# A chunked scan on TensorE: outputs of two chunks at a time, behind every second half tile, with a second weight buffer

## The chip, the cores and the metric

One core of a Trainium2 chip runs the whole kernel. The metric is the device time of one execution in microseconds (us), median of several runs. Lower is better.

## What is computed

The reference is two networks in a row, each of two layers. The change lies in the first layer of the second one, a Mamba-like mixer over T = 768 tokens (256 of a context and 512 of the input), cut into six chunks of 128, for 8 groups of 4 heads of 64. It is run forwards and backwards; per chunk, with `la_cum` the running sum of log decays:

```python
states = jnp.einsum('bcsgn,bcsgr,bcsgrp->bcgrpn', bc, to_end, xc)
...
decay = jnp.exp(jnp.where(causal, seg, -jnp.inf))
cb = jnp.einsum('bclgn,bcsgn->bclsg', cc, bc)
w = cb[..., None] * decay * dtc[:, :, None]
y_diag = jnp.einsum('bclsgr,bcsgrp->bclgrp', w, xc)
y_off = jnp.einsum('bclgn,bcgrpn,bclgr->bclgrp', cc, prev, jnp.exp(la_cum))
return (y_diag + y_off).reshape(xs.shape), final
```

The sum of both directions, plus a skip term, is multiplied by `silu(z)`, normed and multiplied by `out_w`.

## The kernel before

The kernel is written as one hand-ordered program for each engine; semaphores are the only links between them. TensorE (PE), VectorE (DVE), ScalarE (ACT) and GpSimd (POOL) each walk their own list, and an instruction that waits holds up all that is behind it on its engine.

The weights come in tiles of 1 MB. SyncE loads a tile into `wraw`, POOL splits it into a rounded part `whi` (L413) and a rest `wlo` (L417), and PE multiplies with whi-hi, wlo-hi and whi-lo (three matmuls for one product). POOL starts on a buffer when PE reports its old tile as done.

The mixer runs over the groups g: seven in a loop (`pe.Fori(0, GROUPS - 1)`, L1015, and its like on the other engines) and the eighth, `last`, written out. The scan of a group needs few PE instructions between long waits for DVE and ACT, so in the seven looped groups PE puts half tiles of the next group's projections between them. A half tile is 24 matmuls of 384 columns, half of the 768 tokens (`dense`, L825): x0, x1 (two feature blocks of x), b and c, each in two parts. The slots of L974 are, in order, x0 part 1, x1 part 0, x1 part 1, b part 0, b part 1, c part 0, and behind slot c PE does:

- `log_decay(c + 1)` (L939): sums of log decays into banks 4 and 5, once ACT has read those of chunk c;
- `off_part(c + 1)` (L950): the state's contribution into bank 6, once DVE has read that of chunk c (semaphore `offs_r`);
- `y_part(c)` (L954): two turned sums (L960), that is `offs` transposed into bank 7, then eight instructions for the four weighted products (L967), `xcb` against `wdec`, which write 64 partitions each and so have the form 128x64 where all others are 128x128. Bank 7 is used in halves by even and odd chunks.

ACT makes the exponentials of a chunk (`decays`, L1731, eight instructions into `ebuf`), copies finished projections out of PSUM (`copy_in`, L1644 to L1646), takes the tanh of the convolutions (L1650, L1651) and rounds the first and second half of the gated result (`u_hi`, L1739, which waits for the gates of three chunks). Its order is: decays(1), (2), (3), copy_in(1), tanh(0), decays(4), u_hi(0), decays(5), copy_in(2), u_hi(1), and so on.

DVE does per chunk c: `skip(c)` (L2519); `offsets(c)` (L2540 to L2544), which reads bank 6 and ends with the addition that lets PE go on with the off sums of the next chunk and the turned sums of this one; `gate_y(c)` (L2550), which multiplies the finished chunk in bank 7 by z; and `weights(c)` (L2525 the sum of both directions' decays, L2528 times C.B) into the one buffer `wdec`, which must wait for `y_part(c - 1)`. Between these it convolves the next group's projections: `conv_start`, four `conv_tap`s (L2388) and a `silu` (L2402) for each of four blocks b. Then come `u_lo` (L2559) and, in the output stage, `out_add` (L2621) into `oacc`.

Of the kernel before, what the change touches and what calls it, by code (L numbers as in the profile page):

```python
# [20 lines left out]
ALU = mybir.AluOpType  # L21
# [3 lines left out]
P = 128  # L25
# [74 lines left out]
def build(nc, io):  # L100
# [93 lines left out]
    btok = at("btok", 178.375, [P, NC, NS])  # L194
    xte = at("xte", 147.375, [P, NC, 2, HPG, HD])
    wdec = at("wdec", 184.375, [P, HPG, P])
    offs = at("offs", 186.375, [P, 3, HPG, HD])
    stmp = at("stmp", 199.875, [P, HPG, HD])
    acc = at("acc", 189.375, [P, T])
# [292 lines left out]
    def _(pe):  # L492
# [377 lines left out]
        def group(g, last):  # L870
# [83 lines left out]
            def y_part(c):  # L954
# [13 lines left out]
                                       start=False, stop=True, skip_group_check=(b == 1))  # L968
                mm.then_inc(y_ps, 1)

            log_decay(0)
            dense(T_G0 % 2, lambda i: i * TM + P, P, IN, EIGHT, True, 2, None)
            off_part(0)
            for c, (name, part) in enumerate((("x0", 1), ("x1", 0), ("x1", 1), ("b", 0), ("b", 1), ("c", 0))):  # L974
                next_half(name, part)
                if c + 1 < NC:
                    log_decay(c + 1)
                    off_part(c + 1)
                y_part(c)
            next_half("c", 1)  # L980

            k = 1 if last else 3
# [968 lines left out]
    def _(dve):  # L1951
# [516 lines left out]
        def group(g, last):  # L2468
# [46 lines left out]
            def skip(c):  # L2515
                if c:
                    dve.wait_ge(offs_r, g * 6 + c)
                dr = drow[:, bass.ds(g * HPG, HPG)].unsqueeze(2).broadcast_to([P, HPG, HD])
                k(V.tensor_tensor(stmp[:, :, :], x4(c), dr, ALU.mult))  # L2519

            def weights(c):
                dve.wait_ge(ex_r, g * 6 + (c + 1))
                if c:
                    dve.wait_ge(y_ps, g * 6 + c)
                V.tensor_tensor(wdec[:, :, :], ebuf[:, 0, :, :], ebuf[:, 1, :, :], ALU.add).then_inc(W_r, 1)  # L2525
                dve.wait_ge(W_r, g * 12 + 2 * c + 1)
                cb = xcb[:, c, 256:384].unsqueeze(1).broadcast_to([P, HPG, P])
                V.tensor_tensor(wdec[:, :, :], wdec[:, :, :], cb, ALU.mult).then_inc(W_r, 1)  # L2528

            def offsets(c):  # L2530
                dve.wait_ge(off_ps, g * 6 + (c + 1))
# [14 lines left out]
            def gate_y(c):  # L2546
# [4 lines left out]
                                       .rearrange("p (b n) -> p b n", b=2), scalar=0.5, in1=z,  # L2551
                                       op0=ALU.mult, op1=ALU.mult).then_inc(y_rd, 1)

            def u_lo(half):

                dve.wait_ge(uh_r, g * 2 + (half + 1))
# [4 lines left out]
                ins.then_inc(u_r, 1)  # L2561

            s1 = g + 1
            skip(0)
            weights(0)
            z_gate(1)
            dve.wait_ge(z_rd, g * 2 + 2)
            offsets(0)
            skip(1)
            offsets(1)  # L2570
            gate_y(0)
            if not last:
                load_params(s1, k)
            weights(1)
            if not last:
                conv_start(s1, 0, k)
                conv_tap(0, 1, k)
                conv_tap(0, 2, k)
            skip(2)
            offsets(2)  # L2580
            gate_y(1)
            weights(2)
            if not last:
                conv_tap(0, 3, k)
                conv_tap(0, 4, k)
            skip(3)
            offsets(3)
            gate_y(2)
            weights(3)
            if not last:  # L2590
                conv_start(s1, 1, k)
                conv_tap(1, 1, k)
            skip(4)
            offsets(4)
            gate_y(3)
            weights(4)
            if not last:
                silu(s1, 0)
                conv_tap(1, 2, k)
            skip(5)  # L2600
            offsets(5)
            gate_y(4)
            weights(5)
            u_lo(0)
            if not last:
                conv_tap(1, 3, k)
                conv_tap(1, 4, k)
            gate_y(5)
            u_lo(1)
            if not last:  # L2610
                silu(s1, 1)
            blk = g * 10 + (4 if last else 6)

# [471 lines left out]
```

## Time and profile before

| | |
|---|---|
| median of 3 runs | 2378.02 us (2377.7 to 2378.32) |
| the profiled execution | 2376.67 us |
| its span, first to last instruction | 2374.5 us |
| mean granted TensorE clock | 0.995 |
| PE busy | 2300.4 us (97%) |
| DVE busy | 1485.9 us (63%) |
| ACT busy | 757.8 us (32%) |
| POOL busy | 1437.1 us (61%) |
| the chain that ended last | PE 76%, DVE 16% |

A busy PE is one with a matmul under way. In a timeline, a row with a count stands for that many instructions in a row, from the start of the first to the end of the last, and neighbouring matmuls overlap; so the distance of two starts tells what one costs. "[0.28 <-DVE wdec L2528]" is idle time before the instruction and what ended it. The seven looped groups of the mixer take about 90 us each, from 1316 us on; their rows repeat to within some hundredths of a microsecond.

### The profile page before, as it was taken

What the parts mean: (1) busy time and instruction counts of PE and PEld (TensorE: products, weight loads), DVE (VectorE), ACT (ScalarE), POOL (GpSimd) and SP (SyncE); (2) the same over time, 40 slices, a digit from 0 to 9 for tenths busy, and PEclk for the clock granted to TensorE, in tenths of its full rate; (3) what the DMA queues carried; (4) which work ended last, traced back from release to release, by engine and by line L of the source; (5) the groups of instructions that cost most, each with busy time, mean ns of one, the idle gap of its engine ahead of it and who ended that gap; (6) DMA issues with size and microseconds to landing.
All of it is one profiled execution on the core that took longest, in us unless ns stands there. A gap on an engine that the chain in (4) does not pass through costs nothing.

```text
span 2374.5 us, 32220 instructions
## 1 busy us (share of the span) xinstructions
PE 2300.4 (97%) x11638; PEld 1901.1 (80%) x11638; DVE 1485.9 (63%) x1851; ACT 757.8 (32%) x1582; POOL 1437.1 (61%) x1259
## 2 busy tenths in 40 slices
PE   8999999999999999999999999999999998999998
PEld 6768888888777788888878899999999986776447
DVE  7965343444774543343468889789789788536653
ACT  3453210112333420110246333333333333532551
POOL 8737776778776477776876434344344341365885
PEclk9999999999999999999999999999999998999999
DMA  4321434433224033443332111110111112122212
GB/s 167 107 81 71 149 135 147 149 132 123 89 76 129 36 131 135 160 142 132 117 115 107 37 53 35 53 53 35 53 53 35 53 53 83 34 74 76 54 27 71
DMA packets 41596, 211.31 MB, mean 89 GB/s; under 512 B 5408, under 2 KB 9504, under 8 KB 21536
## 3 DMA queue, kind: packets, MB, share of 16 engines
q1 hardware_dynamic: 27456, 164.84, 19.7%
q10 hardware_dynamic: 14048, 45.17, 5.8%
q8 instruction: 67, 1.10, 0.2%
q14 instruction: 25, 0.20, 0.0%
HBM read 197.67 MB, written 7.34 MB: 86 GB/s over the span
## 4 chain that ended last, share of the span: by engine, by line
PE 76%; DVE 16%; issue 3%; ACT 2%; DMA 1%; POOL 1%; ACTq 0%; DVEq 0%; SPq 0%; POOLq 0%
PE ps L528 40%; PE ps L825 14%; PE ps L1077 5%; DVE convd L2388 3%; PE ps L1188 2%; PE ps L1170 1%; PE ps L927 1%; PE ps L1175 1%; DVE wdec L2525 1%; PE ps L622 1%; PE ps L950 1%; DVE convd L2402 1%; PE ps L1133 1%; DVE convd L2384 1%; DVE offs L2542 1%
## 5 line engine op out<-in xcount | busy, mean ns | idle before, releaser
L413 POOL TENSOR_SCALAR whi<-wraw 128x512 fp32r<-128x512 f32 x564 | 386.6, 714 | 869.0 <-PE ps L825 374.3
L417 POOL TENSOR_TENSOR wlo<-wraw,whi 128x512 fp32r<-128x512 f32 x568 | 859.4, 1543 | 0.8 <-ACT whi L1428 0.8
L528 PE MATMUL ps<-uhi,whi 128*128 128x512 f32 x896 | 353.6, 395 | 16.1 <-POOL wlo L390 11.6
L528 PE MATMUL ps<-uhi,wlo 128*128 128x512 f32 x896 | 349.9, 390 | 0.0
L528 PE MATMUL ps<-ulo,whi 128*128 128x512 f32 x896 | 349.8, 390 | 0.0
L825 PE MATMUL ps<-inhi,whi 128*128 128x384 f32 (+1 forms) x784 | 242.8, 344 | 4.3 <-DVE inlo L2343 3.2
L825 PE MATMUL ps<-inlo,whi 128*128 128x384 f32 (+1 forms) x784 | 235.8, 335 | 0.0
L825 PE MATMUL ps<-inhi,wlo 128*128 128x384 f32 (+1 forms) x784 | 235.5, 335 | 0.0
L528 PEld LDWEIGHTS ps<-uhi,whi 128*128 128x128 f32 x896 | 168.8, 188 | 54.8 <-POOL wlo L390 11.6
L528 PE MATMUL ps<-hidhi,whi 128*128 128x512 f32 x512 | 199.4, 390 | 0.0
L528 PE MATMUL ps<-hidlo,whi 128*128 128x512 f32 x512 | 199.4, 390 | 0.0
L528 PE MATMUL ps<-hidhi,wlo 128*128 128x512 f32 x512 | 199.4, 389 | 0.0
L2224 DVE TENSOR_TENSOR h<-h,ps 128x1024 f32<-128x1024 f32 x40 | 48.9, 1221 | 239.3 <-PE ps L528 239.3
L528 PEld LDWEIGHTS ps<-uhi,wlo 128*128 128x128 f32 x896 | 168.8, 188 | 36.0 <-issue 1.4
L528 PEld LDWEIGHTS ps<-ulo,whi 128*128 128x128 f32 x896 | 168.7, 188 | 35.2
L1524 ACT ACTIVATE hsq<-hm 128x1024 f32<-128x1024 f32 x32 | 34.1, 1065 | 488.2 <-DVE hm L2255 488.2
L825 PEld LDWEIGHTS ps<-inhi,whi 128*128 128x128 f32 (+1 forms) x784 | 143.6, 187 | 15.6 <-issue 8.6
L2388 DVE SCALAR_TENSOR_TENSOR convd<-raw,cpg,convd 128x770 f32<-128x770 f32 x128 | 149.7, 1169 | 3.4 <-ACT convd L1631 0.9
L2255 DVE SCALAR_TENSOR_TENSOR hm<-ps,rstd 128x1024 f32<-128x1024 f32 x32 | 39.2, 1225 | 173.3 <-PE ps L528 173.2
L825 PEld LDWEIGHTS ps<-inhi,wlo 128*128 128x128 f32 (+1 forms) x784 | 144.2, 187 | 0.8
L825 PEld LDWEIGHTS ps<-inlo,whi 128*128 128x128 f32 (+1 forms) x784 | 144.1, 187 | 0.6
L1731 ACT ACTIVATE ebuf<-ps,tabg 128x128 f32<-128x128 f32 x384 | 104.4, 387 | 116.8 <-PE ps L939 83.8
(448 smaller groups left out, 4623.0 us busy)
## 6 DMA issues: line engine op xcount, KB each, us to landing
wraw<-in_wstream SPq DMA_DIRECT2D x150, 1024.0 KB, 4.8
modraw<-in_modw ACTq DMA_DIRECT2D x48, 512.0 KB, 3.3
hspill<-hres ACTq DMA_DIRECT2D x1, 3072.0 KB, 9.7
hback<-hspill ACTq DMA_DIRECT2D x1, 3072.0 KB, 10.1
Q<-qrow SPq DMA_DIRECT2D x24, 128.0 KB, 2.3
h<-in_x ACTq DMA_DIRECT2D x2, 1024.0 KB, 5.3
crow<-in_crow ACTq DMA_DIRECT2D x2, 1024.0 KB, 4.9
QL<-qrest SPq DMA_DIRECT2D x14, 128.0 KB, 2.3
```

Of the source, the lines that this page charges most:

```text
L413: pool.tensor_scalar(whi[:, s, c], wraw[:, s, c], 1.0, 0.0, ALU.mult, ALU.add).then_inc(wraw_read, 1)
L417: ins = pool.tensor_tensor(wlo[:, s, c], wraw[:, s, c], whi[:, s, c].bitcast(F32), ALU.subtract)
L528: mm = pe.matmul(ps[:, 2 * bank + m, :], a[:, w, c:c + P], b[:, kb, :], start=(n == 0 and i == 0), stop=(n == KB - 1 and i == 2))
L622: pe.matmul(ps[:, SCORE_BANKS(n)[c], 0:w], q, proj[64 * c:64 * c + 64, K0 + hd, 0:w], start=True, stop=False)
L825: mm = pe.matmul(ps[0:width, q + half, 0:HALF], a[:, s, c:c + width], b[:, kb, half * HALF:(half + 1) * HALF], start=(n == 0), stop=(n == ...
L1077: mm = pe.matmul(ps[:, q + m, :], a[:, k % 2, c:c + P], b[:, kb, t0:t0 + S], start=(kb == 0 and i == 0), stop=(kb == KB - 1 and i == 2))
L1188: mm = pe.matmul(ps[64 * e:64 * e + 64, 2, :], vtok2[:, kb, HD * j:HD * j + HD], pT2[(NC * b + kb) % RING][:, e, :], start=(kb == 0), stop ...
L1524: A(hsq[n % 2][:, :, :], hm[n % 2][:, :, :], ACT.Square).then_inc(L["sqh_r"], 1)
L1731: ins = A(ebuf[:, d, r, :], ps[:, 4 + d, r * P:(r + 1) * P], ACT.Exp, bias=tabg[:, K_NB + 2 * c + d, r:r + 1])
L2224: V.tensor_tensor(h[:, 2 * j:2 * j + 2, :], h[:, 2 * j:2 * j + 2, :], TWO(bank), ALU.add).then_inc(L["h_r"], 1)
L2255: V.scalar_tensor_tensor(out=hm[n % 2][:, :, :], in0=TWO(n % 2), scalar=0.0, in1=rstd2, op0=ALU.max, op1=ALU.mult).then_inc(L["m_r"], 1)
L2388: ins = V.scalar_tensor_tensor(out=o, in0=r[:, n:n + CW], scalar=cpg[:, 6 * b + n:6 * b + n + 1], in1=o, op0=ALU.mult, op1=ALU.add)
```

## The change

In the looped groups PE no longer computes outputs behind every half tile. Behind the slots of the odd chunks (1, 3, 5) it does both chunks of a pair: the four turned sums first (`y_turn`), then the sixteen instructions of weighted products (`y_dec`). A pair fills bank 7, so it waits until the gate of the pair before has been read. The odd chunk's weights have a buffer of their own, `wdec1`, in space that `ul` uses later, so `weights(c)` waits only for the pair before its own. One `gate_pair` of 512 elements per partition takes the place of two `gate_y` of 256. DVE's list gets a new order: `load_params` stands where `gate_y(0)` was; `gate_pair(0)`, `(2)` and `(4)` stand behind `offsets(2)`, behind `offsets(4)` and behind `u_lo(0)`; `silu(s1, 0)` and `conv_tap(1, 2)` move from behind `weights(4)` to ahead of `skip(4)`; `conv_tap(1, 3)` and `(1, 4)` move from behind `u_lo(0)` to ahead of `skip(5)`. ACT's and POOL's lists stay. The last group keeps the old code. The diff, cut by the branch that repeats the old DVE order for the last group:

```diff
     btok = at("btok", 178.375, [P, NC, NS])
     xte = at("xte", 147.375, [P, NC, 2, HPG, HD])
     wdec = at("wdec", 184.375, [P, HPG, P])
+    wdec1 = at("wdec1", 154.875, [P, 2, T])[:, :, 0:2 * P].rearrange("p a (r n) -> p a r n", r=2)
     offs = at("offs", 186.375, [P, 3, HPG, HD])
     stmp = at("stmp", 199.875, [P, HPG, HD])
     acc = at("acc", 189.375, [P, T])
@@ -968,6 +969,34 @@
                                        start=False, stop=True, skip_group_check=(b == 1))
                 mm.then_inc(y_ps, 1)
 
+            def y_turn(c):
+
+                pe.wait_ge(offs_r, g * 6 + (c + 1))
+                for b in range(2):
+                    q = b * 256 + c % 2 * P
+                    pe.matmul(ps[:, 7, q:q + P], offs[:, 2 * (c % 2), 2 * b:2 * b + 2, :].rearrange("p r n -> p (r n)"), ident[:, :],
+                              start=(q == 0), stop=False, skip_group_check=(q > 0), is_transpose=True)
+
+            def y_dec(c):
+
+                pe.wait_ge(W_r, g * 12 + 2 * c + 2)
+                for b in range(2):
+                    q = b * 256 + c % 2 * P
+                    for r in range(2):
+                        x0 = (2 * b + r) * HD
+                        w = wdec1[:, b, r, :] if c % 2 else wdec[:, 2 * b + r, :]
+                        mm = pe.matmul(ps[64 * r:64 * r + 64, 7, q:q + P], xcb[:, c, x0:x0 + HD], w,
+                                       start=False, stop=True, skip_group_check=(q > 0))
+                mm.then_inc(y_ps, 1)
+
+            def y_pair(c):
+
+                pe.wait_ge(y_rd, g * 6 + (6 + c))
+                y_turn(c)
+                y_turn(c + 1)
+                y_dec(c)
+                y_dec(c + 1)
+
             log_decay(0)
             dense(T_G0 % 2, lambda i: i * TM + P, P, IN, EIGHT, True, 2, None)
             off_part(0)
@@ -976,7 +1005,10 @@
                 if c + 1 < NC:
                     log_decay(c + 1)
                     off_part(c + 1)
-                y_part(c)
+                if last:
+                    y_part(c)
+                elif c % 2:
+                    y_pair(c - 1)
             next_half("c", 1)
 
             k = 1 if last else 3
@@ -2520,12 +2552,17 @@
 
             def weights(c):
                 dve.wait_ge(ex_r, g * 6 + (c + 1))
-                if c:
+                if last and c:
                     dve.wait_ge(y_ps, g * 6 + c)
-                V.tensor_tensor(wdec[:, :, :], ebuf[:, 0, :, :], ebuf[:, 1, :, :], ALU.add).then_inc(W_r, 1)
+                elif c > 1:
+                    dve.wait_ge(y_ps, g * 6 + c - 1)
+                own = c % 2 == 0 or last
+                w = wdec[:, :, :].rearrange("p (a r) n -> p a r n", a=2) if own else wdec1
+                e = lambda d: ebuf[:, d, :, :].rearrange("p (a r) n -> p a r n", a=2)
+                V.tensor_tensor(w, e(0), e(1), ALU.add).then_inc(W_r, 1)
                 dve.wait_ge(W_r, g * 12 + 2 * c + 1)
-                cb = xcb[:, c, 256:384].unsqueeze(1).broadcast_to([P, HPG, P])
-                V.tensor_tensor(wdec[:, :, :], wdec[:, :, :], cb, ALU.mult).then_inc(W_r, 1)
+                cb = xcb[:, c, 256:384].unsqueeze(1).unsqueeze(1).broadcast_to([P, 2, 2, P])
+                V.tensor_tensor(w, w, cb, ALU.mult).then_inc(W_r, 1)
 
             def offsets(c):
                 dve.wait_ge(off_ps, g * 6 + (c + 1))
@@ -2551,6 +2588,13 @@
                                        .rearrange("p (b n) -> p b n", b=2), scalar=0.5, in1=z,
                                        op0=ALU.mult, op1=ALU.mult).then_inc(y_rd, 1)
 
+            def gate_pair(c):
+
+                dve.wait_ge(y_ps, g * 6 + (c + 2))
+                z = zs[:, :, c * P:(c + 2) * P]
+                V.scalar_tensor_tensor(out=z, in0=ps[:, 7, :].rearrange("p (b n) -> p b n", b=2), scalar=0.5, in1=z,
+                                       op0=ALU.mult, op1=ALU.mult).then_inc(y_rd, 2)
+
             def u_lo(half):
 
                 dve.wait_ge(uh_r, g * 2 + (half + 1))
@@ -2561,53 +2605,73 @@
                 ins.then_inc(u_r, 1)
 
             s1 = g + 1
...
+            else:
+                skip(0)
+                weights(0)
+                z_gate(1)
+                dve.wait_ge(z_rd, g * 2 + 2)
+                offsets(0)
+                skip(1)
+                offsets(1)
                 load_params(s1, k)
-            weights(1)
-            if not last:
+                weights(1)
                 conv_start(s1, 0, k)
                 conv_tap(0, 1, k)
                 conv_tap(0, 2, k)
-            skip(2)
-            offsets(2)
-            gate_y(1)
-            weights(2)
-            if not last:
+                skip(2)
+                offsets(2)
+                gate_pair(0)
+                weights(2)
                 conv_tap(0, 3, k)
                 conv_tap(0, 4, k)
-            skip(3)
-            offsets(3)
-            gate_y(2)
-            weights(3)
-            if not last:
+                skip(3)
+                offsets(3)
+                weights(3)
                 conv_start(s1, 1, k)
                 conv_tap(1, 1, k)
-            skip(4)
-            offsets(4)
-            gate_y(3)
-            weights(4)
-            if not last:
                 silu(s1, 0)
                 conv_tap(1, 2, k)
-            skip(5)
-            offsets(5)
-            gate_y(4)
-            weights(5)
-            u_lo(0)
-            if not last:
+                skip(4)
+                offsets(4)
+                gate_pair(2)
+                weights(4)
                 conv_tap(1, 3, k)
                 conv_tap(1, 4, k)
-            gate_y(5)
-            u_lo(1)
-            if not last:
+                skip(5)
+                offsets(5)
+                weights(5)
+                u_lo(0)
+                gate_pair(4)
+                u_lo(1)
                 silu(s1, 1)
             blk = g * 10 + (4 if last else 6)
 
```

## Rows read from the trace of the kernel before

**Rows 1.** Waits of PE, 1345 to 1435 us; line <- who was waited for: us, times, longest.

```profile
PE ps L967 <- DVE wdec L2528: 0.3, 1, 0.3
PE ps L825 <- DVE oacc L2621: 0.2, 1, 0.2
```

**Rows 2.** Timeline of PE, second group: start us, us, instruction, count [idle before].

```profile
1435.34 0.38 PE L960 MATMUL ps<-ident,offs 128*128 128x128 f32 x2
...
1436.52 0.34 PE L825 MATMUL ps<-inhi,wlo 128*128 128x384 f32 x1
...
1440.51 0.63 PE L939 MATMUL ps<-lablk,lapick 128*128 128x512 f32 x2
1440.98 1.02 PE L950 MATMUL ps<-ast,ck 128*128 128x256 f32 x4
1441.84 0.38 PE L960 MATMUL ps<-ident,offs 128*128 128x128 f32 x2
1442.15 0.66 PE L967 MATMUL ps<-wdec,xcb 128*64 128x128 f32 x8
1442.74 0.44 PE L825 MATMUL ps<-inhi,whi 128*128 128x384 f32 x1
1443.02 0.34 PE L825 MATMUL ps<-inhi,wlo 128*128 128x384 f32 x1
```

**Rows 3.** Instructions of line L967: count, duration in ns min/median/max, start, forms.

```profile
L967 PE MATMUL ps<-wdec,xcb x384: 272/273/476, 1345.5 to 1994.5; 128*64 128x128 f32 x192
```

**Rows 4.** Timeline of PE, the last weighted products of the second group.

```profile
1466.52 0.38 PE L960 MATMUL ps<-ident,offs 128*128 128x128 f32 x2
1467.18 0.66 PE L967 MATMUL ps<-wdec,xcb 128*64 128x128 f32 x8 [0.28 <-DVE wdec L2528]
```

**Rows 5.** Busy time of each engine in a stretch: us, PE, PEld, DVE, ACT, POOL, clock, DMA.

```profile
1436.88:1467.50 30.62, 30.34 (x190) 27.74 (x191) 29.76 (x43) 12.93 (x45) 10.82 (x9) 1.00 0.20 68
```

**Rows 6.** Timeline of DVE, second group.

```profile
1450.80 0.41 DVE L2550 SCALAR_TENSOR_TENSOR zs<-ps,zs 128x256 f32<-128x256 f32 x1
1451.13 1.45 DVE L2525 TENSOR_TENSOR wdec<-ebuf 128x512 f32<-128x512 f32 x1
1452.62 1.66 DVE L2528 TENSOR_TENSOR wdec<-wdec,xcb 128x512 f32<-128x512 f32 x1
...
1459.48 0.42 DVE L2544 TENSOR_TENSOR offs<-offs,stmp 128x256 f32<-128x256 f32 x1
...
1461.48 0.95 DVE L2402 SCALAR_TENSOR_TENSOR convd<-raw,convd 128x770 f32<-128x770 f32 x1
...
1463.40 0.42 DVE L2519 TENSOR_TENSOR stmp<-xcb,drow 128x256 f32<-128x256 f32 x1
...
1466.43 0.69 DVE L2528 TENSOR_TENSOR wdec<-wdec,xcb 128x512 f32<-128x512 f32 x1
...
1468.10 2.07 DVE L2388 SCALAR_TENSOR_TENSOR convd<-raw,cpg,convd 128x770 f32<-128x770 f32 x2
1470.09 0.42 DVE L2550 SCALAR_TENSOR_TENSOR zs<-ps,zs 128x256 f32<-128x256 f32 x1
```

**Rows 7.** Groups of DVE instructions: count | busy us, mean ns | idle before, releaser.

```profile
L2474 DVE SCALAR_TENSOR_TENSOR zs<-zs,ps 128x768 f32<-128x768 f32 x16 | 15.3, 954 | 30.2 <-ACT zs L1699 30.2
...
L2550 DVE SCALAR_TENSOR_TENSOR zs<-ps,zs 128x256 f32<-128x256 f32 x48 | 19.9, 415 | 0.0
```

**Rows 8.** Timeline of ACT, second group.

```profile
1435.08 0.50 ACT L1646 ACTIVATE raw<-ps 128x384 f32<-128x384 f32 x1
...
1441.26 2.17 ACT L1731 ACTIVATE ebuf<-ps,tabg 128x128 f32<-128x128 f32 x8 [3.62 <-PE ps L939]
...
1456.27 1.17 ACT L1739 ACTIVATE uh<-zs,mng 128x384 fp32r<-128x384 f32 x2
```

**Rows 9.** Timeline of PE in the last group (g = 7).

```profile
1973.23 0.67 PE L950 MATMUL ps<-ast,ck 128*128 128x256 f32 x2 [2.09 <-DVE offs L2544]
```

**Rows 10.** Busy time of each engine in a stretch of the last group.

```profile
1974.80:1978.00 3.20, 3.00 (x7) 1.85 (x8) 3.13 (x5) 0.32 (x2) 3.20 (x3) 0.50 1.00 430
```

More of the change, by code:

```diff
@@ L2563, in group @@
             s1 = g + 1
[L2564 to L2571, printed above, removed]
-            if not last:
+            if last:
+                skip(0)
[5 more added lines that the diff above has]
+                offsets(1)
+                gate_y(0)
+                weights(1)
+                skip(2)
+                offsets(2)
+                gate_y(1)
+                weights(2)
+                skip(3)
+                offsets(3)
+                gate_y(2)
+                weights(3)
+                skip(4)
+                offsets(4)
+                gate_y(3)
+                weights(4)
+                skip(5)
+                offsets(5)
+                gate_y(4)
+                weights(5)
+                u_lo(0)
+                gate_y(5)
+                u_lo(1)
+            else:
+                skip(0)
+                weights(0)
+                z_gate(1)
+                dve.wait_ge(z_rd, g * 2 + 2)
+                offsets(0)
+                skip(1)
+                offsets(1)
                 load_params(s1, k)
-            weights(1)
-            if not last:
+                weights(1)
                 conv_start(s1, 0, k)
@@ L2578, in group @@
                 conv_tap(0, 2, k)
-            skip(2)
-            offsets(2)
-            gate_y(1)
-            weights(2)
-            if not last:
+                skip(2)
+                offsets(2)
+                gate_pair(0)
+                weights(2)
                 conv_tap(0, 3, k)
                 conv_tap(0, 4, k)
-            skip(3)
-            offsets(3)
-            gate_y(2)
-            weights(3)
-            if not last:
+                skip(3)
+                offsets(3)
+                weights(3)
                 conv_start(s1, 1, k)
                 conv_tap(1, 1, k)
-            skip(4)
-            offsets(4)
-            gate_y(3)
-            weights(4)
-            if not last:
                 silu(s1, 0)
                 conv_tap(1, 2, k)
-            skip(5)
-            offsets(5)
-            gate_y(4)
-            weights(5)
-            u_lo(0)
-            if not last:
+                skip(4)
+                offsets(4)
+                gate_pair(2)
+                weights(4)
                 conv_tap(1, 3, k)
                 conv_tap(1, 4, k)
-            gate_y(5)
-            u_lo(1)
-            if not last:
+                skip(5)
+                offsets(5)
+                weights(5)
+                u_lo(0)
+                gate_pair(4)
+                u_lo(1)
                 silu(s1, 1)
```

## The prediction

> **What bounds the kernel now.** The page comes first: TensorE (PE) is busy 97% of the span, so time can only come from work it stops doing, or go into idle time it is given. The waits of PE over one scan iteration are small; two matter here [rows 1]. One is 0.3 us on the second write of `wdec` (L2528): VectorE (DVE) hands over the last chunk's weights just after PE wants them. The timeline of PE gives the rhythm [rows 2]: a half tile of 24 matmuls runs at (1440.51 - 1436.52) / 23 = 0.173 us each, 4.16 us; the decay sums cost 0.47 (L939 to L950) and the two off sums 0.86 (L950 to L960). From 1436.88 to 1467.50 DVE is busy 29.76 of 30.62 us [rows 5]: from `gate_y(0)` to the end of `weights(5)` it does nothing but follow its own list. Two engines are thus both nearly full, and DVE's list ends last [rows 4]. A change that moves DVE work ahead of `weights(5)` is paid by PE.
>
> **PE's part.** No matmul is added or removed. What goes is the change of form between the 128x128 and the 128x64 matmuls. Of one `y_part` [rows 2]: one matmul of 128 columns lasts 0.273 [rows 3]; the two turned sums last 0.38 together, so they start 0.11 apart and need 0.22; the first weighted product starts 0.31 after the first turned sum, 0.09 lost. The eight product instructions last 0.66 together, so they start 0.055 apart, 0.44; the next L825 starts 0.59 after the first, 0.15 lost. The L825 after that comes 0.28 later and not 0.173, 0.11 lost. Lost in all: 0.35 us for each group of products. Three groups instead of six save 3 x 0.35 = 1.05 us per iteration, if PE is what counts. A pair costs 2 x 0.66 + 0.35 = 1.67 us.
>
> **DVE's part.** Compare the two lists up to the end of `weights(5)`.
> - Out: five `gate_y` (chunks 0 to 4). One holds its slot for 1451.13 - 1450.80 = 0.33 us [rows 6], five 1.67.
> - In: two `gate_pair`, 512 elements. The nearest rows are the same operation on 256 elements, 0.415, and one of the same kind on 768, 0.954 [rows 7]: 0.27 per further 256, so the slot is 0.33 + 0.27 = 0.60, two 1.20. Bounds: 0.33 (nothing for the length) and 0.69 with no overlap with the next instruction.
> - In: `conv_tap(1, 3)` and `conv_tap(1, 4)`, which stood behind `weights(5)` and now stand ahead of `skip(5)`: 1470.09 - 1468.10 = 1.99 us [rows 6].
> - `silu(s1, 0)` and `conv_tap(1, 2)` stay ahead of `weights(5)` but now stand ahead of `skip(4)`: nothing for this sum, 1463.40 - 1461.48 = 1.92 for `offsets(4)` [rows 6].
> - The weights go to `wdec` or `wdec1` with the same 512 elements: I take no cost. Bounds 0 and, for a poorer access pattern, 0.05 on each of six instructions (no row shows one; 0.05 is about half of the overlap that a gate has, 0.415 less 0.33).
> Sum: -1.67 + 1.20 + 1.99 = +1.52 us until `weights(5)` is ready. No wait ahead of it is later: the chain is free of PE between those points except where checked below.
>
> **The timeline this makes**, in the second group, that of the rows. After the off sum of chunk 1, PE would go straight on at 1435.34 (where L960 starts now), but x1 writes the bank that ScalarE (ACT) copies out until 1435.08 + 0.50 = 1435.58 [rows 8]: a new wait of 0.3, start 1435.65 with 0.1 for the start. Then half tile 4.16, 1.33 for decay and off sums, pair 1.67, half tile, 1.33, half tile, 1.33, pair, half tile: 1459.7. The pair (2, 3) finds its weights: `weights(3)` ended at 1452.62 + 1.66 = 1454.28 [rows 6], is now 0.4 earlier (three gates out, one pair in), and PE comes to it at about 1454.9.
> Then `off_part(5)`: after 0.47 of L939 PE is there at 1460.2 and waits for `offsets(4)`, which ended at 1459.48 + 0.42 = 1459.90 [rows 6] and now ends at 1459.90 + 1.92 - 3 x 0.33 + 0.60 = 1461.4. **New stall, 1.2 to 1.3 us**, L950 on L2544; queued behind it are `off_part(5)`, the half tile c and everything after. PE leaves at 1461.5, off sums 0.86, c 4.16: 1466.5. That is where it was before (L960 at 1466.52 [rows 4]): the 1.2 us it had gained is gone.
> The pair (4, 5) now waits for `offsets(5)` and then for `weights(5)`: ready before at about 1467.12 (1466.43 + 0.69 [rows 6]), now at 1468.64. PE could take it at 1466.5 + 0.97 = 1467.5. It starts the products of chunk 5 at 1468.70 instead of 1467.18 [rows 4] and the next half tile 1.52 us later than before. ACT's last exponentials don't stand in for this: `u_hi(0)` now waits for `gate_pair(2)` (about 1462.1), its 1.17 and the 2.2 of eight exponentials [rows 8] end at 1465.4, before DVE comes to `weights(5)` at 1467.2.
>
> **Behind the scan.** PE waits 0.2 us for DVE's first sum into `oacc` [rows 1]. `u_lo(1)` and what follows on DVE start when they did before (the taps are done, `gate_pair(4)` starts at about 1469.7, where `gate_y(5)` was at 1470.09), while PE is 1.5 later: this wait goes, 0.18 back. POOL's split of the next tile starts later with PE; `wsplit` is not among PE's waits [rows 1]. The unrolled last group keeps its old order.
> Per iteration 1.52 - 0.18 = +1.34 us, seven iterations 9.4 us. The profiled execution took 2376.67 us (span 2374.5 and 2.2 around it), 1.35 under the median of the three runs: 2376.7 + 9.4 = 2386.1, and against the median **2387.4 us**.
>
> **Clock.** In the last group PE stood idle 2.09 us on this same pair of lines, and 1.6 us later its clock was granted at half, 1.2 GHz, from 1974.8 to 1978.0 [rows 9, 10]. The forecast adds one stall of 1.3 us and two of about 0.6 per iteration. No row of the loop shows so much, so I take no drop. The Trainium skill says (TensorE: Matmul & The Clock Gate, "A second HAM failure mode: psum-queue depth-cycling") that short idle times between groups of matmuls can make the clock swing; the last group agrees with it, and by that rule the second rival below would be the result.
>
> **Rivals.**
> - *Faster: PE's saving counts.* If DVE had `weights(5)` ready by the time PE comes, PE would keep its 1.05 and lose the 0.3 wait of now, less 0.3 for ACT's bank: about 1.0 us per iteration, 2378 - 7 = 2371. It decides where DVE's list is over 1.1 us shorter than I make it and its `offsets(4)` too. For it: PE is 97% busy. Against: two taps of 1.0 each are plainly ahead of the weights. Chance 0.10.
> - *Slower still: the clock drops in the loop.* Some 3.2 us at half clock lose 1.6, of which the later waits may hide 1.1 if it falls early: 0.5 to 1.6 more per iteration, 2391 to 2399, I take 2396. Chance 0.08.
> - *No difference.* The stalls are eaten where PE has other waits, or the idle of PE lets DVE and POOL, which slow each other (L2528 1.66 us at 1452.62, 0.69 at 1466.43 [rows 6]), meet less: with half a microsecond to 1.3 per iteration given back, 2378 to 2382. Chance 0.12.
> - The forecast has 0.70; its own range is 2383 to 2392 (gates and access patterns move 1.34 by -0.5 to +0.7 per iteration).
> The range 2377 to 2396 leaves out the faster rival and the top of the slower one. About 0.2% (4.8 us) is what a measurement can tell from no change: faster 0.10, same 0.12, slower 0.78.
>
> **What would show it.** In the profile after: PE's waits get L950 on DVE L2544 with 1.2 to 1.5 us in each of seven iterations (nothing of the kind before outside the last group), the transposes and products of the last pair wait for `offs` and `wdec` by about 0.6 each, and one wait of 0.3 on the copy L1646 appears; the gaps between forms halve in number; the wait on `oacc` is gone in the loop; each of the seven iterations grows by 1.3 us; the clock stays at 1.00. It is wrong if DVE is idle ahead of `weights(5)`, if the stall before `off_part(5)` is missing, or if `gate_pair` takes much other than 0.68.

## The result, and the profile after

The changed kernel takes 2391.4 us (median of 4 runs, 2389.9 to 2393.5) against 2378.2 before: 1.0056 times as long (95% interval 1.0044 to 1.0068), 13.2 us more, where 9.4 were forecast. The profiled execution took 2390.2 us with a span of 2388.2, 13.7 over the span of before, at a mean granted clock of 0.993. Line numbers shift: L825, L937, L939 and L950 are now L826, L938, L940 and L951; the turned sums are L977, the weighted products L988; on DVE `weights` is L2562 and L2565, `offsets` L2577 to L2581, `gate_pair` L2595, taps L2420, `silu` L2434, `out_add` L2685.

PE's waits in the second group, 1437 to 1527 us (those of [rows 1] are of the first):

```profile
PE ps L951 <- DVE offs L2581: 1.9, 1, 1.9
PE ps L938 <- ACT ast L1754: 0.6, 1, 0.6
PE ps L988 <- DVE wdec L2565: 0.3, 1, 0.3
PE ps L977 <- DVE offs L2581: 0.3, 1, 0.3
```

The 0.6 on L938 was there before (L937). New are the stall before `off_part(5)` and 0.3 on the turned sums; the 0.3 on `wdec` stays; the wait on `oacc` is gone.

The timeline of PE in the first group (as [rows 2, 4]; a start 0.12 lower than before is the same moment, as L940 at 1344.21 and L939 at 1344.33 tell):

```profile
1344.68 0.59 PE L951 MATMUL ps<-ast,ck 128*128 128x256 f32 x2
1345.40 0.44 PE L826 MATMUL ps<-inhi,whi 128*128 128x384 f32 x1
...
1351.00 0.60 PE L977 MATMUL ps<-ident,offs 128*128 128x128 f32 x4
1351.53 1.09 PE L988 MATMUL ps<-wdec,xcb 128*64 128x128 f32 x16
1352.56 0.44 PE L826 MATMUL ps<-inhi,whi 128*128 128x384 f32 x1
...
1372.00 1.10 PE L951 MATMUL ps<-ast,ck 128*128 128x256 f32 x4 [1.90 <-DVE offs L2581]
...
1377.12 0.38 PE L977 MATMUL ps<-ident,offs 128*128 128x128 f32 x2
1377.80 0.44 PE L977 MATMUL ps<-ident,offs 128*128 128x128 f32 x2 [0.30 <-DVE offs L2581]
1378.17 0.66 PE L988 MATMUL ps<-wdec,xcb 128*64 128x128 f32 x8
1379.13 0.66 PE L988 MATMUL ps<-wdec,xcb 128*64 128x128 f32 x8 [0.30 <-DVE wdec L2565]
1379.72 0.44 PE L826 MATMUL ps<-inhi,whi 128*128 128x384 f32 x1
```

The pair starts at 1351.00 and the half tile behind it at 1352.56, 1.56, and its second matmul follows 0.11 late: 1.67. The half tile behind the last products starts at 1379.72. In the kernel before it was this one:

```profile
1377.66 0.44 PE L825 MATMUL ps<-inhi,whi 128*128 128x384 f32 x1
```

so PE is 1379.72 - 1377.66 + 0.12 = 2.18 us late there, not 1.52. The timeline of DVE after, same group (as [rows 6]):

```profile
1346.64 1.26 DVE L2406 COPY cpg<-p 128x24 f32 x1
...
1354.08 0.68 DVE L2595 SCALAR_TENSOR_TENSOR zs<-ps,zs 128x512 f32<-128x512 f32 x1
1354.68 0.68 DVE L2562 TENSOR_TENSOR wdec<-ebuf 128x512 f32<-128x512 f32 x1
...
1360.85 1.78 DVE L2562 TENSOR_TENSOR wdec<-ebuf 128x512 f32<-128x512 f32 x1
1362.66 1.64 DVE L2565 TENSOR_TENSOR wdec<-wdec,xcb 128x512 f32<-128x512 f32 x1
...
1367.86 0.96 DVE L2434 SCALAR_TENSOR_TENSOR convd<-raw,convd 128x770 f32<-128x770 f32 x1
1368.73 1.01 DVE L2420 SCALAR_TENSOR_TENSOR convd<-raw,cpg,convd 128x770 f32<-128x770 f32 x1
...
1378.38 0.69 DVE L2565 TENSOR_TENSOR wdec<-wdec,xcb 128x512 f32<-128x512 f32 x1
```

Beside it the same list of the kernel before, where two gates stand, of chunk 0 and of chunk 2:

```profile
1346.75 0.41 DVE L2550 SCALAR_TENSOR_TENSOR zs<-ps,zs 128x256 f32<-128x256 f32 x1
1347.08 0.94 DVE L2374 COPY cpg<-p 128x24 f32 x1
...
1360.69 0.41 DVE L2550 SCALAR_TENSOR_TENSOR zs<-ps,zs 128x256 f32<-128x256 f32 x1
1361.03 1.44 DVE L2525 TENSOR_TENSOR wdec<-ebuf 128x512 f32<-128x512 f32 x1
1362.50 1.66 DVE L2528 TENSOR_TENSOR wdec<-wdec,xcb 128x512 f32<-128x512 f32 x1
1364.09 1.63 DVE L2384 TENSOR_SCALAR convd<-raw,cpg 128x770 f32<-128x770 f32 x1
1365.75 1.93 DVE L2388 SCALAR_TENSOR_TENSOR convd<-raw,cpg,convd 128x770 f32<-128x770 f32 x1
...
1376.33 0.69 DVE L2528 TENSOR_TENSOR wdec<-wdec,xcb 128x512 f32<-128x512 f32 x1
```

and what POOL does at that time, before (L417) and after (L418):

```profile
1342.43 5.56 POOL L417 TENSOR_TENSOR wlo<-wraw,whi 128x512 fp32r<-128x512 f32 x4
...
1360.47 6.39 POOL L417 TENSOR_TENSOR wlo<-wraw,whi 128x512 fp32r<-128x512 f32 x4
```

```profile
1360.62 6.38 POOL L418 TENSOR_TENSOR wlo<-wraw,whi 128x512 fp32r<-128x512 f32 x4
```

Here is the missing 0.66 us. The `wlo` work of POOL runs in four instructions of 6.39 / 4 = 1.60 us, and meanwhile DVE gets one instruction done for each of them: L2525, L2528, L2384 and the first tap start 1.47, 1.59 and 1.66 apart, though with POOL idle they take 0.7 to 1.0.

The copy of `load_params` ends with POOL's last piece as well (1347.08 + 0.94 = 1348.02 against 1342.43 + 5.56 = 1347.99; after, 1346.64 + 1.26 = 1347.90 against 1347.86). With the gate in front of it taken away, the copy starts 0.32 earlier on the scale of before, lasts 0.32 longer (0.94 to 1.26) and ends where it did. `weights(1)` starts at 1347.94 + 0.12 = 1348.06 where it started at 1348.05.

For chunk 2 the list is already 0.27 late, because the first pair's gate takes 0.60 us in the place of 0.33. L2525 starts at 1360.85 + 0.12 = 1360.97, 0.06 earlier than before, but takes 1.78 instead of 1.44, and L2528 starts 1362.66 + 0.12 - 1362.50 = 0.28 late. So the missing gate of chunk 2 gave nothing back. POOL's pieces begin 1360.62 + 0.12 - 1360.47 = 0.27 later too: the two engines shift together. Of the five gates of 0.33 only three were worth anything.

The Trainium skill has a rule for such pairs (SBUF — State Buffer, "SBUF: two separate sides"): a VectorE operation with two SBUF inputs, while GpSimd reads SBUF, or one in a two-port mode, shares a port pair with GpSimd; whichever starts first holds it for its whole instruction, and the other waits. The rows agree in the pace of `weights` and the tap, one for each piece of 1.60 us. The copy and `conv_start` have one tensor input in SBUF and were held too; whether they ran in such a two-port mode no run here shows.

What the loop costs follows from the distance between the same instruction (L913 before, L914 after) in neighbouring groups: 90.11 us before; 91.84 in five of the seven groups after and 92.43 in two. 5 x 1.73 + 2 x 2.32 = 13.3 of the 13.7 us of span. The two slower groups hold a spell at the lower clock. Here is one of them (columns as in [rows 10]); the other shows 0.57 from 1832 to 1836, and the same place in the second group, 1463 to 1467, shows 1.00:

```profile
1647.00:1651.00 4.00, 3.41 (x10) 3.09 (x11) 3.92 (x6) 2.92 (x10) 0.00 (x0) 0.59 0.00 0
```

### The profile page after: what moved, and what is told of

It reads as the page before. It is cut to its first block, busy times and chain, and to the rows that moved or that the text cites. A ratio compares the mean times of both kernels' runs of the same rounds, so it can differ in the third digit from the quotient of the medians.

```text
span 2388.2 us, 32213 instructions
## 1 busy us (share of the span) xinstructions
PE 2300.0 (96%) x11638; PEld 1903.6 (80%) x11638; DVE 1499.2 (63%) x1830; ACT 758.3 (32%) x1582; POOL 1426.7 (60%) x1259
## 4 chain that ended last, share of the span: by engine, by line
PE 82%; DVE 10%; issue 3%; ACT 2%; POOL 1%; DMA 1%; ACTq 0%; DVEq 0%; SPq 0%; POOLq 0%
PE ps L529 41%; PE ps L826 18%; PE ps L1109 5%; DVE convd L2420 2%; PE ps L1220 2%; PE ps L1202 1%; PE ps L928 1%; PE ps L596 1%; POOL wlo L418 1%; DVE wdec L2562 1%; PE ps L1207 1%; PE ps L623 1%; PE ps L951 1%; PE ps L1165 1%; PE ps L1076 1%
## 5 line engine op out<-in xcount | busy, mean ns | idle before, releaser
L418 POOL TENSOR_TENSOR wlo<-wraw,whi 128x512 fp32r<-128x512 f32 x568 | 849.1, 1527 | 0.8 <-ACT whi L1460 0.8
L826 PE MATMUL ps<-inhi,whi 128*128 128x384 f32 (+1 forms) x784 | 245.0, 347 | 5.2 <-DVE inlo L2375 3.2
L826 PE MATMUL ps<-inhi,wlo 128*128 128x384 f32 (+1 forms) x784 | 236.1, 336 | 0.0
L826 PE MATMUL ps<-inlo,whi 128*128 128x384 f32 (+1 forms) x784 | 236.0, 335 | 0.0
L826 PEld LDWEIGHTS ps<-inhi,whi 128*128 128x128 f32 (+1 forms) x784 | 144.7, 188 | 16.4 <-DVE inlo L2375 5.8
L2420 DVE SCALAR_TENSOR_TENSOR convd<-raw,cpg,convd 128x770 f32<-128x770 f32 x128 | 155.4, 1214 | 3.4 <-ACT convd L1663 0.9
L826 PEld LDWEIGHTS ps<-inhi,wlo 128*128 128x128 f32 (+1 forms) x784 | 145.0, 188 | 1.3
L826 PEld LDWEIGHTS ps<-inlo,whi 128*128 128x128 f32 (+1 forms) x784 | 144.7, 187 | 0.6
```

The costliest lines, as they stand in the source:

```text
L418: ins = pool.tensor_tensor(wlo[:, s, c], wraw[:, s, c], whi[:, s, c].bitcast(F32), ALU.subtract)
L826: mm = pe.matmul(ps[0:width, q + half, 0:HALF], a[:, s, c:c + width], b[:, kb, half * HALF:(half + 1) * HALF], start=(n == 0), stop=(n == ...
L2420: ins = V.scalar_tensor_tensor(out=o, in0=r[:, n:n + CW], scalar=cpg[:, 6 * b + n:6 * b + n + 1], in1=o, op0=ALU.mult, op1=ALU.add)
```

## The experiments

Each ratio is against runs of the kernel before on the same chip, which took 2378.1 us beside all but the last three kernels and 2376.8 beside those. "Period" is the distance between neighbouring looped groups in the profiled execution.

**The moved convolution steps alone.** The kernel before, with its gates and single outputs, and only the four steps moved.

```diff
+                silu(s1, 0)
+                conv_tap(1, 2, k)
             skip(4)
             offsets(4)
             gate_y(3)
             weights(4)
             if not last:
-                silu(s1, 0)
-                conv_tap(1, 2, k)
+                conv_tap(1, 3, k)
+                conv_tap(1, 4, k)
             skip(5)
...
             u_lo(0)
-            if not last:
-                conv_tap(1, 3, k)
-                conv_tap(1, 4, k)
             gate_y(5)
```

> The kernel before with single outputs, but with the four conv steps moved as in the change: silu(s1, 0) and conv_tap(1, 2) ahead of skip(4), conv_tap(1, 3) and (1, 4) ahead of skip(5). Theory, VectorE's list ends last: weights(5) is 1.99 us later, PE gets back 0.47 behind the scan, so +1.5 us per looped group, about 2378 + 11 = 2389, perhaps 1 more where the clock falls. Rival, the pairing itself is what costs (its wait for a whole bank, its stalls): within 2 us of 2378.

Measured: 2388.5 us, ratio 1.0042 (1.0029 to 1.0056); period 91.65, +1.53. PE's waits in the second group:

```profile
PE ps L950 <- DVE offs L2544: 1.3, 1, 1.3
PE ps L967 <- DVE wdec L2528: 0.6, 2, 0.4
```

So 1.53 of the 1.73 us a group come without any pair, as expected. The two taps are the term, 1.99 less 0.46 given back behind the scan: 1.53. With these four steps moved, the pairs then add 91.84 - 91.65 = 0.19. A stall of 1.3 us came in each group and the clock did not fall in the loop.

**The pairs alone.** The change, with the four steps back where they stood.

```diff
-                silu(s1, 0)
-                conv_tap(1, 2, k)
                 skip(4)
                 offsets(4)
                 gate_pair(2)
                 weights(4)
-                conv_tap(1, 3, k)
-                conv_tap(1, 4, k)
+                silu(s1, 0)
+                conv_tap(1, 2, k)
                 skip(5)
                 offsets(5)
                 weights(5)
                 u_lo(0)
+                conv_tap(1, 3, k)
+                conv_tap(1, 4, k)
                 gate_pair(4)
```

> The changed kernel with pairs, second buffer and pair gates, but all four conv steps back at their old places. Theory: weights(5) only 0.2 us later than in the kernel before (three gates of 0.33 out, two pair gates of 0.60 in), PE bound to it as before: 2378 to 2380; the saving of PE between forms doesn't show. Rival 1, PE's saving counts: 2378 - 7 = 2371. Rival 2, the pairing costs: 2389 or more.

Measured: 2388.3 us, ratio 1.0046 (1.0032 to 1.0059); period 91.59. A miss by 8 us; the rival that the pairing costs (2389 or more) came nearer. `weights(5)` ends 0.16 late, close to the 0.2 of the sum, and the half tile behind it starts 0.16 late. The rest comes behind the scan, a wait on `oacc` seven times as long as before ([rows 1]):

```profile
PE ps L826 <- DVE oacc L2685: 1.5, 1, 1.5
```

The timeline of DVE there (starts 0.79 higher than before are the same moment), below it that of the kernel before, and last that of the change (0.12 lower):

```profile
1382.81 1.51 DVE L2603 SCALAR_TENSOR_TENSOR ul<-zs,mng,uh 128x384 fp32r<-128x384 f32 x2 [1.19 <-ACT uh L1771]
...
1386.53 3.21 DVE L2420 SCALAR_TENSOR_TENSOR convd<-raw,cpg,convd 128x770 f32<-128x770 f32 x2
1389.87 0.96 DVE L2685 TENSOR_TENSOR oacc<-oacc,ps 128x768 f32<-128x768 f32 x1
```

```profile
1381.59 1.15 DVE L2559 SCALAR_TENSOR_TENSOR ul<-zs,mng,uh 128x384 fp32r<-128x384 f32 x2 [1.19 <-ACT uh L1739]
...
1384.96 2.53 DVE L2388 SCALAR_TENSOR_TENSOR convd<-raw,cpg,convd 128x770 f32<-128x770 f32 x2
1387.63 0.95 DVE L2621 TENSOR_TENSOR oacc<-oacc,ps 128x768 f32<-128x768 f32 x1
```

```profile
1381.93 1.15 DVE L2603 SCALAR_TENSOR_TENSOR ul<-zs,mng,uh 128x384 fp32r<-128x384 f32 x2 [1.19 <-ACT uh L1771]
...
1384.58 2.54 DVE L2420 SCALAR_TENSOR_TENSOR convd<-raw,cpg,convd 128x770 f32<-128x770 f32 x2
1387.37 0.95 DVE L2685 TENSOR_TENSOR oacc<-oacc,ps 128x768 f32<-128x768 f32 x1 [0.26 <-PE ps L826]
```

The gate of the last pair is 0.27 longer and the scan 0.16 later, so `u_lo(1)` starts 1382.81 - 0.79 - 1381.59 = 0.43 late. It takes 1.51 instead of 1.15, and the two taps, which meet POOL's next `wlo` pieces (2.0 us each), last 3.21 instead of 2.53. The first sum starts 1389.87 - 0.79 - 1387.63 = 1.45 late. The pairs spare DVE nothing that counts there, and the list behind the scan had no slack: its wait of 0.2 said so.

In the change `u_lo(1)` is just as late, 1381.93 + 0.12 - 1381.59 = 0.46. But PE comes to its output stage 2.0 us later than here, and POOL, which starts its next split when PE reports, starts at 1384.49 on the scale of before where it started at 1382.45 here. `u_lo(1)`, `silu`, `conv_start` and the two taps then take 1.15, 0.95, 0.68 and 2.54 us, where here they take 1.51, 1.36, 0.97 and 3.21, and the first sum waits for PE. So it is PE's own lateness that took the wait on `oacc` away, and not an earlier list of DVE. The two halves don't add up (1.48 and 1.53 give 1.73 together), since PE pays for one late list at one place or the other.

**`silu` and one tap back, the last two taps left in front.**

```diff
-                silu(s1, 0)
-                conv_tap(1, 2, k)
                 skip(4)
                 offsets(4)
                 gate_pair(2)
                 weights(4)
+                silu(s1, 0)
+                conv_tap(1, 2, k)
                 conv_tap(1, 3, k)
```

> The changed kernel with only silu(s1, 0) and conv_tap(1, 2) back behind weights(4); conv_tap(1, 3) and (1, 4) stay ahead of skip(5). Theory: the 1.9 us stall of PE ahead of off_part(5) goes, but weights(5) comes at the same time, so PE waits there instead: 1.74 us per group as in the changed kernel, less the two clock drops of 0.58: 2390. Rival, the stall ahead of off_part(5) is the cost: 7 x 1.9 = 13 us less, 2378.

Measured: 2393.2 us, ratio 1.0066 (1.0052 to 1.008), 3 us over the forecast, which took no spells at half clock. The stall before `off_part(5)` is gone and stands whole before the turned sums of chunk 5:

```profile
PE ps L977 <- DVE offs L2581: 2.2, 1, 2.2
```

The period is 91.84 in four groups, the same as after the change to the hundredth, so the place of the stall doesn't matter: the end of `weights(5)` does. Three groups have a spell at half clock (the clock was 0.57 in 1379 to 1383) and take 92.8 to 92.9.

**Are the gates of chunks 0 and 2 free?** The kernel before, with the first put behind the held copy and the second behind both instructions of `weights(3)`. (In the last group both stay where they were; those lines of the edit are left out.)

```diff
-            gate_y(0)
             if not last:
                 load_params(s1, k)
+                gate_y(0)
...
-            gate_y(2)
             weights(3)
             if not last:
+                gate_y(2)
```

> The kernel before with two instructions of VectorE swapped in order, no work changed: gate_y(0) behind load_params in place of ahead of it, gate_y(2) behind weights(3) in place of ahead of it. Theory, the copy of load_params and the first sum of weights(3) are held until an instruction of POOL ends, so a gate ahead of them is free and one behind them costs 0.33: +0.66 us per looped group for weights(5), 7 x 0.66 = +4.6, about 2383. Rival, POOL only slows what runs beside it and order doesn't matter: 2378, within 1 us.

Measured: 2381.5 us, ratio 1.0016 (1.0007 to 1.0025); period 90.64, +0.53. The timeline of DVE:

```profile
1348.31 1.26 DVE L2374 COPY cpg<-p 128x24 f32 x1
1349.60 0.42 DVE L2550 SCALAR_TENSOR_TENSOR zs<-ps,zs 128x256 f32<-128x256 f32 x1
```

No work is added, the copy is 0.32 longer and everything behind the gate is 0.34 late: for chunk 0 the gate was free where it stood. For chunk 2 the test isn't clean: `y_part(3)` now waits 1.1 us for the late gate, and POOL's pieces fall on other instructions. L2525 went from 1.44 to 1.78 here too, but it starts 1.12 us later than before, so it is not the same meeting. `weights(5)` ends 0.50 late, between the 0.33 of one free gate and the 0.66 of two. For chunk 2 the rows of the change above are the better evidence.

**One sum earlier.** The pairs alone, with `out_add(0)` one tap earlier.

```diff
                 conv_tap(2, 1, k)
-                conv_tap(2, 2, k)
                 out_add(0)
+                conv_tap(2, 2, k)
                 conv_tap(2, 3, k)
```

> Pairs with the four conv steps at their old places, as in e2_pairs_conv_back (2388.3 us, 1.49 us idle per group before PE's fourth output block, waiting for VectorE's first sum into oacc), and now that first sum stands one conv tap earlier. Theory, only the lateness of that sum made the run before slow: the idle goes, 91.6 per group falls to 90.0 to 90.2, 2377 to 2379. Rival, the loss is somewhere else and only shows there: 2386 to 2388.

Measured: 2387.9 us, ratio 1.0042 (1.0027 to 1.0057); period 91.53. A miss: the wait of 1.4 us went to the next sum, which stands behind two taps of 2.98 us. A single place was not the cause; the list as a whole is late.

**The list behind the scan in another order, with pairs and without.** From `weights(5)` on, the taps 2 to 4 of block 1 go behind the last gate, the sums go one or two steps forward each, and the last three taps of block 3 behind the last sum. Once on the changed kernel, whose edit follows (cut behind the third sum), and once on the kernel before (with its `gate_y`s).

```diff
-                silu(s1, 0)
-                conv_tap(1, 2, k)
                 skip(4)
                 offsets(4)
                 gate_pair(2)
                 weights(4)
-                conv_tap(1, 3, k)
-                conv_tap(1, 4, k)
+                silu(s1, 0)
                 skip(5)
                 offsets(5)
                 weights(5)
                 u_lo(0)
                 gate_pair(4)
+                conv_tap(1, 2, k)
+                conv_tap(1, 3, k)
+                conv_tap(1, 4, k)
                 u_lo(1)
...
                 conv_start(s1, 2, k)
+                out_add(0)
                 conv_tap(2, 1, k)
+                out_add(1)
                 conv_tap(2, 2, k)
-                out_add(0)
+                out_add(2)
```

> Pairs with VectorE's list put in another order: conv_tap(1, 2), (1, 3) and (1, 4) between gate_pair(4) and u_lo(1), silu(s1, 0) behind weights(4), each sum into oacc one or two conv steps earlier. Theory: weights(5) is ready before PE comes, so PE keeps its 1.05 us between forms, less 0.3 for ACT's bank, and the wait for oacc of 0.47 goes: 88.8 to 89.2 per group, 2378 - 7 x 1.1 = 2370. Rival, VectorE's whole list is the bound and an order can't help: 2378 or more.

> The kernel before, single outputs, with the same new order of the conv steps and sums as e6_pairs_rebalanced. Theory: the waits for weights(5) (0.28) and for oacc (0.47) go, the form changes stay: 89.3 to 89.5 per group, 2378 - 7 x 0.7 = 2373; so e6 less e7 is what the pairing itself gives, 2 to 4 us. Rival, the pairing gives nothing: e6 and e7 within 1 us.

Measured: with pairs 2369.2 us, ratio 0.9962 (0.9948 to 0.9976), period 88.83; with single outputs 2370.4 us, ratio 0.9967 (0.9956 to 0.9978), period 89.27. In both, one wait of PE is left in a group, the 0.6 us for ACT that was there before.

So DVE's list bounds the kernel before and the changed one, and it is its order that decides. With one tap fewer ahead of `weights(5)` than even the kernel before, PE sets the pace almost alone, and the pairs are worth 0.44 a group. Almost: with pairs `off_part(5)` still starts 0.57 us behind its decay sums (1372.71 to 1373.28) where 0.47 is usual. Which of the two moves, the taps or the sums, brought how much was not tried. The whole times don't tell the two kernels apart, their intervals overlap: the first group of the profiled execution with pairs came 2.8 us later (L914 at 1328.41, L913 at 1325.59), by what happened ahead of the loop. The period does: it repeats to some hundredths from group to group in both.

**POOL's pieces halved.** The kernel before; in the scan's loop POOL writes `wlo` in eight instructions of 256 columns.

```diff
-                    ins = pool.tensor_tensor(wlo[:, s, c], wraw[:, s, c], whi[:, s, c].bitcast(F32), ALU.subtract)
+                    for m in range(parts):
+                        w = TILE // PIECES // parts
+                        c = slice((n * parts + m) * w, (n * parts + m + 1) * w)
+                        ins = pool.tensor_tensor(wlo[:, s, c], wraw[:, s, c], whi[:, s, c].bitcast(F32), ALU.subtract)
...
-            split_pair(i)
+            split_pair(i, parts=2)
```

> The kernel before with one change on POOL: in the scan's loop the rest of a tile (wlo) is made in eight instructions of 256 columns, not four of 512. Theory, an instruction of VectorE with two SBUF inputs is held until POOL's instruction beside it ends, one for each: four of them that take 1.45 to 1.93 us now take 0.8 to 1.2, weights(5) is ready some 2 us earlier, the two waits of 0.28 and 0.47 go: 2378 - 5 = 2373. Rival, they share a path in proportion and the size of a piece doesn't matter: 2378.

Measured: 2371.9 us, ratio 0.9972 (0.9962 to 0.9981), period 89.26. The timelines of DVE and POOL, second group (as [rows 6]):

```profile
1452.26 0.89 DVE L2528 TENSOR_TENSOR wdec<-ebuf 128x512 f32<-128x512 f32 x1
1453.18 1.11 DVE L2531 TENSOR_TENSOR wdec<-wdec,xcb 128x512 f32<-128x512 f32 x1
1454.22 1.10 DVE L2387 TENSOR_SCALAR convd<-raw,cpg 128x770 f32<-128x770 f32 x1
1455.35 1.37 DVE L2391 SCALAR_TENSOR_TENSOR convd<-raw,cpg,convd 128x770 f32<-128x770 f32 x1
```

```profile
1451.69 8.08 POOL L420 TENSOR_TENSOR wlo<-wraw,whi 128x256 fp32r<-128x256 f32 x8
```

The same four operations that took 1.45, 1.66, 1.63 and 1.93 take 0.89, 1.11, 1.10 and 1.37, in the rhythm of POOL's pieces of 8.08 / 8 = 1.01 us. POOL is slower in all (8.1 instead of 6.4 us), which nobody waits for. Because it works longer, three more operations of DVE meet it (`skip(4)` and two of `offsets(4)`, 0.83 to 0.84 us where they took 0.43), so `weights(5)` ends 0.88 us earlier and not the 2 us of the forecast. That was enough: both waits are gone. The length of POOL's instruction is what DVE pays.

**Halves with the change, and with both other orders.**

> The changed kernel as it is, with POOL's rest of a tile in eight instructions of 256 columns in the scan's loop. Theory: weights(5) comes about 1.0 us earlier, as it did in e8_pool_halves, of the 2.17 that it came later by the change: 91.84 per group falls to about 90.8, the stall ahead of off_part(5) from 1.9 to 0.9, no clock drops in the loop: 2383. Rival, the stalls and not VectorE's list set the time: 2390.

> Pairs in the new order of e6_pairs_rebalanced (88.83 per group, 2369.2) with POOL's halves on top. Theory: PE has no wait on VectorE left there, so a shorter list of VectorE brings nothing: 88.8 per group, 2369. Rival, both add up: 2363 to 2366.

> Singles in the new order of e7_singles_rebalanced (89.27 per group, 2370.4) with POOL's halves on top. Theory: 89.27 again, and 0.44 more per group than e10: pairing gives 7 x 0.44 = 3 us where PE is the bound. Rival, pairing gives nothing: equal to e10.

Each is the kernel of the section above with the edit of POOL's pieces. Measured: the change 2385.6 us, ratio 1.0035 (1.0022 to 1.0047), period 91.60 (90.93 in the first group); reordered pairs 2366.0, ratio 0.9957 (0.9943 to 0.997), period 88.63; reordered single outputs 2369.4, ratio 0.9973 (0.9961 to 0.9985), period 89.28. For the change the gain is smaller than expected, 0.24 a group where 1.0 was forecast, and the stall before `off_part(5)` falls from 1.9 to 1.0 in the first group only, to 1.7 in the others: its `silu` and `conv_tap(1, 2)` stand where POOL's pieces, longer by then in all, still run, and take 1.38 and 1.49 us where they took 0.96 and 1.01:

```profile
1459.37 1.38 DVE L2437 SCALAR_TENSOR_TENSOR convd<-raw,convd 128x770 f32<-128x770 f32 x1
1460.67 1.49 DVE L2423 SCALAR_TENSOR_TENSOR convd<-raw,cpg,convd 128x770 f32<-128x770 f32 x1
```

The pair of reordered kernels gives the cleanest price of the pairs: no wait of PE on DVE in either, 89.28 - 88.63 = 0.65 us a group. For the single outputs halving brings nothing (89.27 and 89.28): PE was already the bound. For the pairs it brings 0.20, where nothing was forecast: `off_part(5)` starts 0.47 behind its decay sums again, and from there to the turned sums it is 5.03 us instead of 5.13. The reordered pairs with halves are the fastest version found, 0.43% under the kernel before beside them.

## Why the prediction was right, and where it was off

**The direction and its reason: right.** DVE's list sets the end of `weights(5)`, two taps stand ahead of it that didn't, and what PE saves is lost at the next wait. The moved steps alone cost 1.53 of the 1.73 a group. The pairs alone cost 1.48, at a second place where DVE's list has no slack, the first sum into `oacc`; in the change it stays hidden behind the loss at `weights(5)`. The reordered kernels, which ease both, show the saving.

**PE's part: right.** A pair of 1.67 us was forecast and measured. So was the wait of 0.3 before x1: L951 to L826 is 0.72 us in the rows above, where two such off sums need 0.43 (1344.80 to 1345.23 in the kernel before); it is hidden from the list of waits because PE is still finishing a matmul. 3 x 0.35 - 0.3 = 0.75 should come in where PE is the bound; 0.65 did, with POOL's halves.

**`gate_pair`: right.** 0.68 long, and it holds DVE for 1354.68 - 1354.08 = 0.60.

**The sum on DVE: the term "five gates out" was mis-sized.** It counted 5 x 0.33. Two of the five stood ahead of an instruction that POOL held anyway. With three gates the sum is -1.00 + 1.20 + 1.99 = +2.19; 2.18 was measured. The prediction had the rows for it, L2528 at 1.66 beside 0.69 in [rows 6], and used them only as an argument for the rival of no difference. It read DVE's 29.76 busy of 30.62 us as its own list alone [rows 5], but four operations in it last 1.45, 1.66, 1.63 and 1.93 where they take 0.68, 0.69, 0.68 and 1.02 with POOL idle: 3.6 us of that busy time is being held. The stall before `off_part(5)` was forecast at 1.2 to 1.3 from the same sum; with one gate fewer taken off for chunk 2 and one for chunk 0 it is 1.9, as measured. The bounds missed the cause. What they name upwards is 2 x (0.69 - 0.60) + 6 x 0.05 = 0.48, not the +0.7 that the range takes; with 0.48 it would end at 2390.8, under the 2391.4 measured. That the result lies inside the forecast's own range of 2383 to 2392 is in part luck.

**The waits at the turned sums and the products of the last pair: about right.** Forecast were 0.6 each. The view of waits shows 0.30 each, but from start to start the turned sums of chunk 5 are 1377.80 - 1377.12 - 0.22 = 0.46 late and its products 1379.13 - 1378.17 - 0.44 = 0.52.

**Behind the scan: 0.18 given back was forecast, 0.46 came.** [rows 1] shows 0.2 of idle time, but these are the matmuls around that wait in the kernel before:

```profile
1387.92 0.51 PE L825 MATMUL ps<-ul,whi 128*128 128x384 f32 x2
1388.64 0.63 PE L825 MATMUL ps<-uh,whi 128*128 128x384 f32 x2 [0.21 <-DVE oacc L2621]
```

They start 0.72 apart where 0.35 is usual, and the next comes 0.10 late besides: 0.47. The view of waits shows idle time only after the last matmul has ended; the start-to-start distance holds the whole loss. The reason given, that DVE's list starts there when it did, was off: `u_lo(1)` is 0.46 late, and POOL's later split makes up for it.

**The clock: no drop was forecast in the loop; two of seven groups had one, 0.58 us each.** The rival's mechanism thus came in for a small part, in the one profiled execution. The other executions of this kernel spread over 3.6 us. The page of the Trainium skill named in the prediction (TensorE: Matmul & The Clock Gate, "A second HAM failure mode: psum-queue depth-cycling") tells of such swings behind short idle times. The two spells agree with it; the five groups with the same stall and no spell show that the stall alone does not decide.

**The whole:** forecast 7 x (1.52 - 0.18) = 9.4. Measured 7 x (2.18 - 0.46) = 12.0, and 2 x 0.58 = 1.2 for the clock: 13.2. Two misses of opposite sign, 0.66 and 0.28 a group, make 2.7 of the 3.8 us between forecast and result; the clock makes the rest.

**The rivals.** "PE's saving counts" is false for this kernel and true for the reordered one, by the condition it named: DVE's list more than 1.1 us shorter up to `weights(5)`. "No difference" is false. Less meeting between DVE and POOL was its ground: behind the scan they did meet less, which only took the 0.46 away, and in the scan it is just this meeting that made the result worse.

Open: why the clock fell in some groups with the same stall and not in others. The second free gate is shown by the starts in the change's own trace and by the sum, not by an experiment that moves it alone.

## What to carry to other kernels

When work is taken out of an engine's list, ask for each piece whether the instruction behind it could have started earlier to any use: one that another engine holds absorbs the saving, while what is added costs in full. Before merging outputs to save TensorE's changes of form, see which engine ends last before each wait; with the same order of VectorE's list on both sides, the merge here loses 1.48 us a group in the old order and 0.19 in that of the change, and gains 0.44 (0.65 with short pieces of POOL) in the third. The order itself was worth more than the merge (0.84 a group on the kernel before). Long GpSimd instructions beside a busy VectorE list are worth cutting: the same work in twice as many instructions gave 0.3%. And look behind the change for what now starts later: here a late TensorE held back GpSimd, and that gave VectorE its speed back where TensorE no longer needed it.

## What the hardware showed

- VectorE instructions that read SBUF alone (`weights`, `conv_start`, taps, the small copy) run one for each GpSimd instruction while GpSimd subtracts from SBUF: 1.45 to 1.93 us beside pieces of 1.60, 0.89 to 1.37 beside pieces of 1.01, 0.68 to 1.02 alone. Gates and output sums, which read PSUM and SBUF, keep their 0.41 and 0.95 us. GpSimd pays too: a piece of 512 columns took 1.39 us with little beside it and 1.60 in the middle of the scan.
- TensorE's granted clock fell to 0.50 (1.2 GHz; 1648 to 1650 in the change) behind some of the stalls of like length and not behind others. Per looped group, in one profiled execution of each kernel: no drop in seven with stalls of 1.3 us, none in fourteen with 1.4 and 1.5 (before the output sums), none in seven with 1.0 to 1.7, two in seven with 1.9, three in seven with 2.2. A spell cost 0.6 us behind the stall before `off_part(5)` and 0.9 to 1.0 behind that before the turned sums.
- A stall that the view of waits shows as 0.2 us cost PE 0.47 from start to start, and one of 0.1 to 0.3 was not shown at all (`off_part(5)` in the reordered pairs, the half tile of x1).
